# Moving operands of the large matmuls at one address modulo 256, in a two-block transformer kernel on one core

## The chip, the core and the metric

The kernel runs on one core of a Trainium2 chip. A core has TensorE (matmuls), VectorE, ScalarE, GpSimd, SyncE and 16 DMA engines. The metric is the time of one execution on the device, in microseconds (us).

## What is computed

Two blocks follow each other, all in float32. The input x is 256 rows of 2048. Both blocks, cut to what matters:

```python
# first block
mod = silu(c) @ w_ada + b_ada;  shift, scale, gate = split(mod, 3)
h = rms_norm(x, g_norm) * (1 + scale) + shift
qa, ka, va, za, q_idx, k_idx, w_idx, qb, kb, vb, zb = split(h @ w_in)   # 9296 columns
ya = selected_attention(qa, ka, va, q_idx, k_idx, w_idx)                 # top 64 keys
yb = causal_attention(qb, kb, vb)
y = concat(ya * silu(za), yb * silu(zb)) @ w_out
x = x + gate * y
# second block: 16 rows of meta tokens go ahead of x
z = rmsnorm(r, mix_pre_g) @ w_in_2 + b_in_2                              # 8200 columns
q, k, v, f_logit, u, g_attn, g_pool = split(z)
attn = forgetting_attention(q, k, v, log_sigmoid(f_logit))
pool = multiscale_pool(u, pool_w, pool_scale)
m = sigmoid(g_attn) * (attn @ w_attn_o) + sigmoid(g_pool) * (pool @ w_pool_o)
r = r + rmsnorm(m @ w_out_2, mix_post_g)
a = causal_dwconv(rmsnorm(r, ffn_pre_g) @ w_ffn_up, conv_w, conv_b)      # 3 taps, 2 x 5632
r = r + rmsnorm((gelu(gate) * val) @ w_ffn_down, ffn_post_g)             # gate, val = split(a)
out = r[16:]
```

The weights are 96 million numbers, 383 MB, and each is read once.

## The kernel before

**Activations are kept transposed**: a chunk holds 128 of the 2048 features on the partitions, and the rows of the sequence as columns. The first block works on SEQ = 256 columns, the second on ROWS = 272 (with the meta tokens) and, where the convolution's reach is all that is needed, on LIVE = 258, from column LIVE0 = 14 on.

**Each large product is done in three matmuls** of the type float32r. Weights and activations are split in a high part, which that type holds exactly, and the low rest. Lines 753 to 755 are the inner loop of `panel` in `pe_program`:

```python
pe.matmul(out, w_lo, a_hi, start=c == 0, stop=False)
pe.matmul(out, w_hi, a_lo, start=False, stop=False)
ins = pe.matmul(out, w_hi, a_hi, start=False, stop=last)
```

The weights are the stationary operand (128 x 128), the activations the moving one, of 256, 272 or 258 columns of 4 bytes. A **job** is one product. It has n panels of 512 output columns, and a panel has J pieces of weights, each 128 x 1024 (two chunks k of the contraction by 512 columns). For one piece, `panel` goes over four banks of PSUM (M.acc), and in each over the two chunks with three matmuls each: a panel of 16 chunks has 192 matmuls. The jobs in order: qidx0, strip, qidx1, qk_a, v_a, qk_b, v_b, z_a, z_b, out_a, out_b (256 columns); qkv2, f2, u2 (272); g2, attn_o, pool_w, attn_o3, pool_o, out2, up (258); down. The matmuls of pool_w are written out on lines 1053 to 1055. Between the pieces of qk_a to z_b and of g2 stand the small matmuls and transposes of the attention.

**The pieces** come by SyncE's DMAs into four tiles raw, in turn. ScalarE copies one to w_hi (line 1170), VectorE subtracts it for w_lo (line 1660), and TensorE gives the slot back when the piece is done. Semaphores count all of this; the order on each engine is written out by hand.

**The last product, down**, is the other way round: the activations (d_hi, d_lo) are stationary and the weight tiles move, with 512 columns, on lines 1121 to 1123 of `down_panel`.

**Where operands lie.** `memory` gives each tile its byte offset in a partition. What is worked out from it, modulo 256:

| tile | start | pitch of a chunk | chunks at, modulo 256 |
|---|---|---|---|
| w_hi, w_lo (four each) | 128 | 512 per bank, 2048 per k | 128 |
| act_hi, act_lo (all jobs but those below) | 128 | 1088 (272 columns) | 128, 192, 0, 64 in turn |
| the same, read by g2 from column 14 | 184 | 1088 | 184, 248, 56, 120 in turn |
| ya_hi, ya_lo (job out_a) | 64 | 1024 | 64 |
| o_hi / o_lo (attn_o, attn_o3) | 64 / 128 | 1032 | 8 more from chunk to chunk |
| down_hi, down_lo (job down, stationary) | 64 | 512 per matmul | 64 |

The pitch of act_hi is that of 272 columns in all jobs, whatever a job's own width.

Of the kernel before, what the change touches and what calls it, by code (L numbers as in the profile page):

```python
# [28 lines left out]
P = 128  # L29
# [22 lines left out]
PANEL = 512  # L52
POOL_WINDOWS = (2, 4, 8, 16)
# [103 lines left out]
def memory(nc, ctx, A):  # L157
# [50 lines left out]
    q0 = at["o"]  # L208
    M.region = q0


    ada_at = q0
# [46 lines left out]
    x += 16 * LIVE * 4 + 64  # L259
    x = (x + 31) // 32 * 32  # L260
# [14 lines left out]
    M.e8 = put("head_row", [HEADS, P], offset=z + 12288)  # L275
    M.fx = put("log_f", [HEADS, 2 * ROWS], offset=z + 12800)
# [126 lines left out]
    def act(k, c0=0, n=SEQ):  # L403
        return M.act_hi[:, ROWS * k + c0:ROWS * k + c0 + n], M.act_lo[:, ROWS * k + c0:ROWS * k + c0 + n]
# [11 lines left out]
    def attn(k):  # L416
# [726 lines left out]
def act_program(M, act):  # L1143
# [118 lines left out]
    def hi_of(k, c0=0, n=SEQ):  # L1262
        return M.act_hi[:, ROWS * k + c0:ROWS * k + c0 + n]
# [138 lines left out]
    def live_rstd(sem, count, src, c0, n):  # L1402
        def go():
# [5 lines left out]
                         "qkv2", ht(ROWS), lambda c: hi_of(c, 0, ROWS), source=32))  # L1409
# [237 lines left out]
def dve_program(M, dve):  # L1647
# [519 lines left out]
```

## Time and profile before

| | us |
|---|---|
| median of 3 runs | 2143.71 (2142.81 to 2145.34) |
| span of the profiled execution | 2141.7 |
| TensorE busy | 2010.6 (94%), 15084 matmuls |
| VectorE busy | 1282.3 (60%) |
| ScalarE busy | 991.1 (46%) |
| DMA | 391.62 MB, 183 GB/s on average |

The profile comes from one execution. Its rows are groups of instructions by source line, with the number of instructions, their busy time and the mean time of one. A matmul's duration runs from its start to its (modelled) end; matmuls overlap each other, so the time that one costs is the distance from its start to the next one's, and not its duration. "PE" is TensorE, "DVE" VectorE, "ACT" ScalarE, "SP" SyncE. Tile names come without their numbers.

### The profile page before, as it was taken

How to read it: one execution, taken by the hardware profiler on the slowest of the kernel's cores; microseconds unless marked ns; L12 is line 12 of the kernel's file. 1: busy time of each engine (PE TensorE's matmuls, PEld its weight loads, DVE VectorE, ACT ScalarE, POOL GpSimd, SP SyncE). 2: the span in 40 equal slices, each digit the busy share in tenths (PEclk: the TensorE clock that was granted, in tenths of full speed). 3: DMA queues.
4: the chain of work that ended last, by engine and by line, in shares of the span. 5: the costliest groups of instructions: out<-in, count | busy, mean ns of one | idle time of the engine just before them, and what ended most of it. 6: DMA issues, size and time to landing. Idle time of an engine off the chain costs nothing.

```text
span 2141.7 us, 39022 instructions
## 1 busy us (share of the span) xinstructions
PE 2010.6 (94%) x15084; PEld 1911.8 (89%) x15084; DVE 1282.3 (60%) x1565; ACT 991.1 (46%) x1429; POOL 143.8 (7%) x151
## 2 busy tenths in 40 slices
PE   4169999999999999999999999799999999999997
PEld 2169999999999899988899999699999999988886
DVE  6777885685567633444447664666556666664555
ACT  3034555554554444444344444454444444444443
POOL 0000000000002000000004111100000000000000
PEclk8579999999999999999999999899999999999999
DMA  8868665475555555644444555255655665665553
GB/s 308 307 192 286 224 196 175 137 251 182 158 168 188 156 171 157 185 145 138 146 137 142 189 189 179 78 177 174 189 178 175 185 186 177 189 204 189 193 190 124
DMA packets 179903, 391.62 MB, mean 183 GB/s; under 512 B 11955, under 2 KB 17632, under 8 KB 177376
## 3 DMA queue, kind: packets, MB, share of 16 engines
q1 hardware_dynamic: 178800, 388.03, 57.0%
q10 hardware_dynamic: 1024, 2.51, 0.3%
q8 instruction: 54, 0.88, 0.2%
q14 instruction: 25, 0.20, 0.0%
HBM read 388.39 MB, written 2.10 MB: 182 GB/s over the span
## 4 chain that ended last, share of the span: by engine, by line
PE 89%; DVE 4%; DMA 4%; ACT 2%; issue 1%; DVEq 0%; SPq 0%; POOLq 0%; POOL 0%; ACTq 0%
PE acc L753 20%; PE acc L755 20%; PE acc L754 20%; DMA raw<-in_w_ada 4%; PE psum_y L754 2%; PE psum_y L755 2%; PE psum_x L754 2%; PE psum_x L755 2%; PE psum_y L753 2%; PE psum_x L753 2%; PE acc L1123 2%; PE acc L1122 2%; PE acc L1121 2%; PE psum_y L1123 1%; PE psum_x L1123 1%
## 5 line engine op out<-in xcount | busy, mean ns | idle before, releaser
L1660 DVE TENSOR_TENSOR w_lo<-raw,w_hi 128x1024 fp32r<-128x1024 f32 (+1 forms) x644 | 814.0, 1271 | 727.2 <-ACT w_hi L1170 723.9
L1170 ACT ACTIVATE w_hi<-raw 128x1024 fp32r<-128x1024 f32 (+1 forms) x644 | 675.2, 1050 | 929.1 <-PE acc L755 602.4
L753 PE MATMUL acc<-act_hi,w_lo 128*128 128x258 f32 (+2 forms) x3424 | 983.5, 287 | 16.9 <-issue 9.3
L755 PE MATMUL acc<-act_hi,w_hi 128*128 128x258 f32 (+2 forms) x3424 | 974.9, 285 | 0.0
L754 PE MATMUL acc<-act_lo,w_hi 128*128 128x258 f32 (+2 forms) x3424 | 972.8, 284 | 0.0
L753 PEld LDWEIGHTS acc<-act_hi,w_lo 128*128 128x128 f32 x3424 | 651.9, 190 | 27.7 <-issue 26.2
L754 PEld LDWEIGHTS acc<-act_lo,w_hi 128*128 128x128 f32 x3424 | 650.4, 190 | 0.7 <-issue 0.5
L755 PEld LDWEIGHTS acc<-act_hi,w_hi 128*128 128x128 f32 x3424 | 650.7, 190 | 0.0
L754 PE MATMUL psum_y<-act_lo,w_hi 128*128 128x258 f32 x352 | 100.1, 284 | 0.0
L755 PE MATMUL psum_y<-act_hi,w_hi 128*128 128x258 f32 x352 | 100.0, 284 | 0.0
L754 PE MATMUL psum_x<-act_lo,w_hi 128*128 128x258 f32 x352 | 99.8, 284 | 0.0
L755 PE MATMUL psum_x<-act_hi,w_hi 128*128 128x258 f32 x352 | 99.8, 283 | 0.0
L753 PE MATMUL psum_y<-act_hi,w_lo 128*128 128x258 f32 x352 | 99.4, 282 | 0.0
L753 PE MATMUL psum_x<-act_hi,w_lo 128*128 128x258 f32 x352 | 99.3, 282 | 0.0
L1123 PE MATMUL acc<-w_hi,down_hi 128*128 128x512 f32 x176 | 69.3, 394 | 0.0
L1122 PE MATMUL acc<-w_lo,down_hi 128*128 128x512 f32 x176 | 69.0, 392 | 0.0
L1121 PE MATMUL acc<-w_hi,down_lo 128*128 128x512 f32 x176 | 68.3, 388 | 0.0
L716 POOL TENSOR_TENSOR ffn_act<-gelu_gate,conv_val 128x1024 f32 x11 | 34.5, 3135 | 503.5 <-DVE conv_val L1654 503.5
L753 PEld LDWEIGHTS psum_y<-act_hi,w_lo 128*128 128x128 f32 x352 | 67.2, 191 | 0.0
L755 PEld LDWEIGHTS psum_y<-act_hi,w_hi 128*128 128x128 f32 x352 | 66.9, 190 | 0.0
L754 PEld LDWEIGHTS psum_y<-act_lo,w_hi 128*128 128x128 f32 x352 | 66.8, 190 | 0.0
L755 PEld LDWEIGHTS psum_x<-act_hi,w_hi 128*128 128x128 f32 x352 | 66.8, 190 | 0.0
(291 smaller groups left out, 2186.6 us busy)
## 6 DMA issues: line engine op xcount, KB each, us to landing
raw<-in_w_in SPq DMA_DIRECT2D x272, 512.0 KB, 3.6
raw<-in_w_ffn_up SPq DMA_DIRECT2D x176, 512.0 KB, 3.9
raw<-in_w_ffn_down SPq DMA_DIRECT2D x88, 512.0 KB, 3.5
raw<-in_w_ada SPq DMA_DIRECT2D x64, 512.0 KB, 5.2
raw<-in_w_out SPq DMA_DIRECT2D x64, 512.0 KB, 4.1
ada_x<-in_w_ada SPq DMA_DIRECT2D x16, 1024.0 KB, 7.3
raw<-in_w_attn_o SPq DMA_DIRECT2D x16, 512.0 KB, 3.6
raw<-in_w_pool_o SPq DMA_DIRECT2D x16, 512.0 KB, 4.4
```

The lines of the kernel that those rows point to most:

```text
L716: pool.tensor_tensor(M.F[:, ds(i * 4 * SEQ, 4 * SEQ)], M.gg[:, :], M.vt[:, :], ALU.mult).then_inc(M.F_ready, 1)
L753: pe.matmul(out, w_lo, a_hi, start=c == 0, stop=False)
L754: pe.matmul(out, w_hi, a_lo, start=False, stop=False)
L755: ins = pe.matmul(out, w_hi, a_hi, start=False, stop=last)
L1121: pe.matmul(out, d_lo, w_hi, start=start, stop=False)
L1122: pe.matmul(out, d_hi, w_lo, start=False, stop=False)
L1123: ins = pe.matmul(out, d_hi, w_hi, start=False, stop=stop)
L1170: act.activation(M.hi[s][:, 0:job.width], M.raw[s][:, 0:job.width], ACT.Copy).then_inc(M.hi_ready[s], 1)
L1660: dve.tensor_tensor(M.lo[s][:, 0:job.width], M.raw[s][:, 0:job.width], M.hi[s][:, 0:job.width].bitcast(FP32), ALU.subtract).then_inc(M.lo_ ...
```

## The change

Only addresses change; every engine has the same instructions, in the same order, with the same waits. The activations no longer lie ahead of the constants but behind them, at the next offset that is 64 modulo 256. There are two layouts of the same space: act_hi and act_lo with a pitch of 1024 for the first block, act2_hi and act2_lo with a pitch of 320 columns, 1280 bytes, for the second. The stationary tiles of down move from 64 to 192 modulo 256. To make room, head_row and log_f move into parts of o_hi and o_lo. The scratch tiles of the second block shift by 64 bytes modulo 256 with that. g2 still reads its chunks from column 14 on.

```diff
+LINE = 256
+MOVING = 64
+STILL = 192
+PITCH = 320
...
-    act_at = at["o"]
-    M.act_hi = put("act_hi", [P, DC * ROWS], F32R)
-    M.act_lo = put("act_lo", [P, DC * ROWS], F32R)
-    M.ada_first = put("ada_first", [P, D], offset=act_at)
...
-    q0 = at["o"]
-    M.region = q0
-
-
-    ada_at = q0
+    act_at = (at["o"] + LINE - 1 - MOVING % LINE) // LINE * LINE + MOVING % LINE
+    M.act_hi = put("act_hi", [P, DC * SEQ], F32R, act_at)
+    M.act_lo = put("act_lo", [P, DC * SEQ], F32R, act_at + DC * SEQ * 4)
+    M.act2_hi = put("act2_hi", [P, DC * PITCH], F32R, act_at)
+    M.act2_lo = put("act2_lo", [P, DC * PITCH], F32R, act_at + DC * PITCH * 4)
+    M.ada_first = put("ada_first", [P, D], offset=act_at)
+
+
+    ada_at = act_at + 2 * DC * SEQ * 4
+    q0 = act_at + 2 * DC * PITCH * 4
...
-    x += 16 * LIVE * 4 + 64
-    x = (x + 31) // 32 * 32
+    M.e8 = put("head_row", [HEADS, P], offset=x + 6 * LIVE * 4 + 16)
+    M.fx = put("log_f", [HEADS, 2 * ROWS], offset=x + 14 * LIVE * 4 + 16)
+    x = (x + 14 * LIVE * 4 + 16 + 2 * ROWS * 4 + 31) // 32 * 32
...
-    M.d_hi = put("down_hi", [P, 4 * SEQ], F32R, x + 24576)
-    M.d_lo = put("down_lo", [P, 4 * SEQ], F32R, x + 28672)
-    x += 32768
+    d_at = x + 24576
+    d_at += (STILL - d_at) % LINE
+    M.d_hi = put("down_hi", [P, 4 * SEQ], F32R, d_at)
+    M.d_lo = put("down_lo", [P, 4 * SEQ], F32R, d_at + 4096)
+    x = d_at + 8192
...
-    def act(k, c0=0, n=SEQ):
-        return M.act_hi[:, ROWS * k + c0:ROWS * k + c0 + n], M.act_lo[:, ROWS * k + c0:ROWS * k + c0 + n]
+    def act(k):
+        return M.act_hi[:, SEQ * k:SEQ * k + SEQ], M.act_lo[:, SEQ * k:SEQ * k + SEQ]
+
+    def act2(k, c0, n):
+        return M.act2_hi[:, PITCH * k + c0:PITCH * k + c0 + n], M.act2_lo[:, PITCH * k + c0:PITCH * k + c0 + n]
...
-        Job("qkv2", 6, 8, cols(w_in2, 0), lambda k: act(k, 0, ROWS), ROWS),
+        Job("qkv2", 6, 8, cols(w_in2, 0), lambda k: act2(k, 0, ROWS), ROWS),
...
-        Job("g2", 8, 8, cols(w_in2, 4096 + HEADS), lambda k: act(k, LIVE0, LIVE), LIVE),
+        Job("g2", 8, 8, cols(w_in2, 4096 + HEADS), lambda k: act2(k, LIVE0, LIVE), LIVE),
...
-        Job("up", 22, 8, None, lambda k: act(k, 0, LIVE), LIVE),
+        Job("up", 22, 8, None, lambda k: act2(k, 0, LIVE), LIVE),
```

The other jobs of the second block, and the steps of ScalarE and VectorE that write the activations, take act2 in the same way.

## Rows read from the trace of the kernel before

**Rows 1.** The chain that ended last: shares of the span by engine.

```profile
PE 89%; DVE 4%; DMA 4%; ACT 2%; issue 1%; DVEq 0%; SPq 0%; POOLq 0%; POOL 0%; ACTq 0%
```

**Rows 2.** Windows: length, busy (instructions) of PE, PEld, DVE, ACT, POOL; PEclk, DMA, GB/s.

```profile
128.00:701.00 573.00, 568.02 (x4613) 551.62 (x4614) 392.60 (x516) 303.42 (x454) 33.22 (x33) 0.99 0.60 194
...
709.00:912.00 203.00, 202.24 (x1591) 201.86 (x1591) 93.18 (x98) 93.70 (x118) 4.34 (x10) 0.99 0.56 166
912.00:1151.00 239.00, 239.00 (x1782) 213.78 (x1782) 115.05 (x183) 102.55 (x176) 10.11 (x23) 1.00 0.48 142
...
1342.00:1370.00 28.00, 14.94 (x53) 11.34 (x53) 17.40 (x20) 12.76 (x32) 6.29 (x2) 0.73 0.15 49
1370.00:1886.00 516.00, 516.00 (x4256) 516.00 (x4256) 318.31 (x373) 250.49 (x298) 31.34 (x10) 1.00 0.59 179
```

**Rows 3.** Tile ya_hi: duration ns least/median/most, first and last start, forms.

```profile
L755 PE MATMUL acc<-ya_hi,w_hi x128: 276/276/276, 612.5 to 655.7; 128*128 128x256 f32 x128
```

**Rows 4.** Tile act_hi from 655.7 to 701.5 us (out_b), same columns.

```profile
L755 PE MATMUL acc<-act_hi,w_hi x128: 276/282/288, 656.0 to 701.1; 128*128 128x256 f32 x128
```

**Rows 5.** Groups of PE by shape: count, busy us, mean ns.

```profile
L754 PE MATMUL acc<-act_lo,w_hi 128*128 128x258 f32 x1600 | 454.7, 284 | 0.0
...
L754 PE MATMUL acc<-act_lo,w_hi 128*128 128x256 f32 x1296 | 365.3, 282 | 0.0
...
L754 PE MATMUL acc<-act_lo,w_hi 128*128 128x272 f32 x528 | 152.8, 289 | 0.0
L754 PE MATMUL psum_y<-act_lo,w_hi 128*128 128x258 f32 x352 | 100.1, 284 | 0.0
...
L754 PE MATMUL psum_x<-act_lo,w_hi 128*128 128x258 f32 x352 | 99.8, 284 | 0.0
```

**Rows 6.** Windows of TensorE alone: length, busy (instructions), granted clock, DMA, GB/s.

```profile
720.00:840.00 120.00, 120.00 (x955) 1.00 0.59 173
1500.00:1700.00 200.00, 200.00 (x1657) 1.00 0.61 183
1892.00:2118.00 226.00, 226.00 (x989) 1.00 0.55 188
```

**Rows 7.** Groups at 1501.67 us, job up: a chunk at 64; order 753, 754, 755.

```profile
L755 PE MATMUL psum_x<-act_hi,w_hi 128*128 128x258 f32 x1 | 0.3, 289 | 0.0
L754 PE MATMUL psum_x<-act_lo,w_hi 128*128 128x258 f32 x1 | 0.3, 283 | 0.0
L753 PE MATMUL psum_x<-act_hi,w_lo 128*128 128x258 f32 x1 | 0.3, 276 | 0.0
```

**Rows 8.** Groups at 1501.31 us, the chunk at 0 ahead of it.

```profile
L754 PE MATMUL psum_x<-act_lo,w_hi 128*128 128x258 f32 x1 | 0.3, 292 | 0.0
```

**Rows 9.** Line 754 in 1430:1530 and in 720:840 us: duration ns least/median/most.

```profile
L754 PE MATMUL acc<-act_lo,w_hi x149: 280/283/292, 1429.8 to 1529.8; 128*128 128x258 f32 x149
L754 PE MATMUL acc<-act_lo,w_hi x319: 282/287/293, 719.8 to 840.0; 128*128 128x272 f32 x160
```

**Rows 10.** Groups of PE: job down in its first banks.

```profile
L1123 PE MATMUL acc<-w_hi,down_hi 128*128 128x512 f32 x176 | 69.3, 394 | 0.0
L1122 PE MATMUL acc<-w_lo,down_hi 128*128 128x512 f32 x176 | 69.0, 392 | 0.0
L1121 PE MATMUL acc<-w_hi,down_lo 128*128 128x512 f32 x176 | 68.3, 388 | 0.0
L1123 PE MATMUL psum_y<-w_hi,down_hi 128*128 128x512 f32 x88 | 34.7, 394 | 0.0
L1123 PE MATMUL psum_x<-w_hi,down_hi 128*128 128x512 f32 x88 | 34.7, 394 | 0.0
```

**Rows 11.** Waits of TensorE: us in total, times, longest.

```profile
PE acc L753 <- DVE act_lo L1654: 5.7, 5, 3.8
...
PE psum_x L764 <- DVE prob L1848: 1.7, 3, 0.7
```

**Rows 12.** Timeline of TensorE: start us, duration us.

```profile
1501.42 0.28 PE L753 MATMUL psum_x<-act_hi,w_lo 128*128 128x258 f32 x1
1501.53 0.28 PE L754 MATMUL psum_x<-act_lo,w_hi 128*128 128x258 f32 x1
1501.65 0.29 PE L755 MATMUL psum_x<-act_hi,w_hi 128*128 128x258 f32 x1
1501.78 0.29 PE L753 MATMUL psum_y<-act_hi,w_lo 128*128 128x258 f32 x1
```

More of the change, by code:

```diff
@@ L432, in memory @@
         Job("out_b", 4, 4, cols(w_out, 0, 4), act, SEQ),
-        Job("qkv2", 6, 8, cols(w_in2, 0), lambda k: act(k, 0, ROWS), ROWS),
-        Job("f2", 1, 4, lambda i, j: w_in2_s[j][:, :, 3072:3200], lambda k: act(k, 0, ROWS), ROWS,
+        Job("qkv2", 6, 8, cols(w_in2, 0), lambda k: act2(k, 0, ROWS), ROWS),
+        Job("f2", 1, 4, lambda i, j: w_in2_s[j][:, :, 3072:3200], lambda k: act2(k, 0, ROWS), ROWS,
             4, 128, (3,)),
-        Job("u2", 2, 8, cols(w_in2, 3072 + HEADS), lambda k: act(k, 0, ROWS), ROWS),
-        Job("g2", 8, 8, cols(w_in2, 4096 + HEADS), lambda k: act(k, LIVE0, LIVE), LIVE),
+        Job("u2", 2, 8, cols(w_in2, 3072 + HEADS), lambda k: act2(k, 0, ROWS), ROWS),
+        Job("g2", 8, 8, cols(w_in2, 4096 + HEADS), lambda k: act2(k, LIVE0, LIVE), LIVE),
         Job("attn_o", 3, 4, cols(w_ao, 0), attn, LIVE),
-        Job("pool_w", 1, 4, lambda i, j: pool_w[j], lambda k: act(k, 0, LIVE), LIVE, 2, 256),
+        Job("pool_w", 1, 4, lambda i, j: pool_w[j], lambda k: act2(k, 0, LIVE), LIVE, 2, 256),
         Job("attn_o3", 1, 4, cols(w_ao, 3 * PANEL), attn, LIVE),
-        Job("pool_o", 4, 4, cols(w_po, 0), lambda k: act(8 + k, 0, LIVE), LIVE),
-        Job("out2", 4, 8, cols(w_out2, 0), lambda k: act(k, 0, LIVE), LIVE),
-        Job("up", 22, 8, None, lambda k: act(k, 0, LIVE), LIVE),
+        Job("pool_o", 4, 4, cols(w_po, 0), lambda k: act2(8 + k, 0, LIVE), LIVE),
+        Job("out2", 4, 8, cols(w_out2, 0), lambda k: act2(k, 0, LIVE), LIVE),
+        Job("up", 22, 8, None, lambda k: act2(k, 0, LIVE), LIVE),
         Job("down", 11, 8, lambda i, j: down[i, j // 2, j % 2], None, 512, 1, 1024, ()),
@@ L1260, in act_program, with hi_of, hi2_of @@
     ch.step(act.activation(M.bgate[:, :], M.c2[:, V2_UG + 8:V2_UG + 40], ACT.Copy, scale=0.5), wait=False)
-    def hi_of(k, c0=0, n=SEQ):
-        return M.act_hi[:, ROWS * k + c0:ROWS * k + c0 + n]
+    def hi_of(k):
+        return M.act_hi[:, SEQ * k:SEQ * k + SEQ]
+    def hi2_of(k, n):
+        return M.act2_hi[:, PITCH * k:PITCH * k + n]
     def stored(job, i, tile, func=ACT.Copy, squares=None):
@@ L1530, in act_program @@
     mx = pairs(8, "out2", lambda c: M.G[:, c * LIVE:(c + 1) * LIVE],
-               lambda c: hi_of(c, 0, LIVE), source=None, waits=m_done, scale=0.5)
+               lambda c: hi2_of(c, LIVE), source=None, waits=m_done, scale=0.5)
     panel(po, po.n - 1, {n: [mx[n]] for n in range(4)})
@@ L1700, in dve_program @@
     sq = lambda c: M.sq[:, (c % 4) * SEQ:(c % 4 + 1) * SEQ]
-    part_hi = lambda k, n=SEQ: M.act_hi[:, ROWS * k:ROWS * k + n].bitcast(FP32)
-    part_lo = lambda k, n=SEQ: M.act_lo[:, ROWS * k:ROWS * k + n]
+    part_hi = lambda k: M.act_hi[:, SEQ * k:SEQ * k + SEQ].bitcast(FP32)
+    part_lo = lambda k: M.act_lo[:, SEQ * k:SEQ * k + SEQ]
+    part2_hi = lambda k, n: M.act2_hi[:, PITCH * k:PITCH * k + n].bitcast(FP32)
+    part2_lo = lambda k, n: M.act2_lo[:, PITCH * k:PITCH * k + n]
     ch.step(dve.memset(M.ada_first[:, :], 0.0), wait=False)
```

20 lines of the change are left out of this document (9 added, 11 removed).

## The prediction

> **What bounds the kernel now.** I read the chain that ended last first: 89% of it is TensorE [rows 1]. Then the stages in a table of windows: from 128 us to the end of the last projection at 2127 us TensorE is busy nearly without a gap, at the full granted clock, while VectorE, ScalarE and the DMA engines work 60%, 50% and 60% of the time [rows 2]. No instruction is added, removed or reordered by the change, so what it can move is how fast one matmul follows another.
>
> The profile says what that spacing is. In the first half of the output projection (job out_a) the 128 matmuls of line 755 start from 612.5 to 655.7 us; between first and last lie 127 times three matmuls, so one takes 43.2 / 381 = 113.4 ns, and every one has a duration of 276 ns, least and most alike [rows 3]. The second half (out_b) runs the same loop over the same weight matrix, with the same 256 columns, and needs 45.1 / 381 = 118.4 ns, with durations from 276 to 288 [rows 4]. What differs in the code is where the moving operand lies. ya_hi and ya_lo start at 64 bytes modulo 256 and have a pitch of 1024, so each chunk is at 64. act_hi and act_lo start at 128 with a pitch of 1088, so chunk k is at 128, 192, 0, 64 in turn. The stationary operand is at 128 in both. I take this pair as the price of the address.
>
> The other widths, from counts per window (less what was under way at the left edge): 272 columns 120 us / 953 = 125.9 ns, 258 columns 200 / 1655 = 120.8 ns, 512 columns 226 / 988 = 228.7 ns [rows 6]. A duration exceeds its own spacing by about 163 ns (276 against 113.4), so durations in a small window show the spacing of single matmuls.
>
> **A rule against it.** The rows above say that 5 ns hang on the address alone. The Trainium skill says otherwise: its page "SBUF — State Buffer", section "Who interferes with whom", has it that "PE and ACT never wait on anyone", and "TensorE: Matmul & The Clock Gate", section "Step-by-step: what each phase is for", that loading the next weights takes no read bandwidth from the running matmul. By these an address would cost nothing and the sum below would be zero. The trace disagrees, with 276 ns at one address and 276 to 288 at the others.
>
> **Part by part.**
>
> (A) 256 columns, jobs qidx0 to z_b and out_b: pitch 1024, all chunks at 64. That is out_a's case exactly, stationary operand included. Lines 753 to 755 have 1296 each, 3888 in all [rows 5]. The 192 of qidx0 are fed by VectorE step by step (it waits 5.7 us for act_lo there [rows 11]) and gain nothing: 3696 x (118.4 - 113.4) = **18.5 us**. Bounds: none below 15 if the softmax steps between the panels take back some. TensorE's waits for them are 1.7 us now [rows 11], which speaks for the full sum. Above: 19.4.
>
> (B) 272 columns, jobs qkv2, f2, u2: pitch 1280, all at 64: 3 x 528 = 1584 matmuls [rows 5]. The clean value worked out from out_a is 113.4 + 16 columns at 2.4 GHz = 120.1 ns. A 272-column matmul can come that low: the least duration of line 754 is 282 ns (276 + 6.7 is 282.7), its median 287 [rows 9]. 1584 x (125.9 - 120.1) = **9.2 us**; the lower bound is 2 us, if only one in four or five becomes clean.
>
> (C) 258 columns at 64: jobs pool_w, pool_o, out2 and up. The rows of line 754 with this form count 1600 + 352 + 352; less 512 of g2 and with 16 of pool_w on a line of its own that is 1808, times three 5424 matmuls [rows 5]. This is the term on which the result hangs, since a clean value of 113.4 + 0.8 = 114.2 ns would give 5424 x 6.6 = 35.8 us. The trace has this very case already in every fourth chunk (act at 64, weights at 128), and there it isn't clean throughout: the three matmuls of such a chunk take 276, 283 and 289 ns [rows 7], from 1501.42 to the next start at 1501.78, 0.36 us for the three [rows 12]. A chunk at 0 has up to 292 ns [rows 8]. The last of the three may suffer from the next chunk's address, and the first gain from the one before; the middle one has neighbours at 64 on both sides, as in out_a, and takes 283 where out_a's takes 276. It is no exception: of 149 matmuls of line 754 with 258 columns, a quarter of them at 64, none was under 280 ns [rows 9]. Two columns more than 256 seem to cost a step of their own. Its start and the next are 1501.53 and 1501.65 [rows 12], and 283 less 163 is 120, so I take 119.5 ns: 5424 x 1.3 = **7.1 us**. Ends for the range: 114.2 ns (35.8 us) and no gain.
>
> (D) 512 columns, job down: the moving operand is the weight tile, at 128 as before; the stationary one goes from 64 to 192. Line 1123 has 176 + 88 + 88, and with its two sisters that is 1056 [rows 10]. In out_a moving minus stationary is 64 - 128 = -64. Here it is +64 now and becomes 128 - 192 = -64. If only the difference counts, a matmul takes out_a's 113.4 plus 256 columns at 2.4 GHz, 220.1 ns: 1056 x (228.7 - 220.1) = **9.1 us**. Durations of 388 to 394 ns with nothing below [rows 10], where 276 + 106.7 would be 383, say that none is clean now. No row shows a stationary operand at 192, so the bounds are 0 and 9.1. I take the full value, by analogy with out_a alone.
>
> (E) Job g2 reads its chunks from column 14 on, so they lie at 64 + 56 = 120 and not at 64: 1536 matmuls. Before, a quarter of them lay at 120 as well, and the median of all 258-column rows is the same 283 ns [rows 9]. I take nothing, with bounds of 5 us either way. attn_o keeps its pitch of 1032: nothing.
>
> (F) Moved tiles: constants now lie ahead of the activations, head_row and log_f inside o_hi and o_lo. Waits and their order are unchanged, so nothing. The cover: when TensorE takes 1 to 5% less per panel, the weight pieces must come as much faster. With VectorE at 62% and the DMA engines at 59% in the longest stage [rows 2] they do. What lies ahead of 128 us and the stall at 1342 to 1370 us stay as they are.
>
> **Sum:** 18.5 + 9.2 + 7.1 + 9.1 = 43.9 us. The profiled execution has a span of 2141.7 us, the median of the runs is 2143.7; taking the sum from either, with the 2.0 us outside the span kept, gives **2100 us**.
>
> **The rivals.**
>
> R1, 258 columns run clean as well, because the 283 and 289 are remnants of the chunk at 0 ahead and of the one behind, and only a long run at one address settles. For it: out_a settles in one state, and 276 does occur for 258 columns. Against it: the middle one. 43.9 + 28.7 = 72.6 us, 2071 us. Chance 0.22.
>
> R2, only the exact case of out_a gains: (A) 18.5 and a part of (B) and (D), 258 columns nothing. 15 to 30 us, around 2120 us. Chance 0.14.
>
> R3, the address isn't the cause: out_a is clean for another reason (what the other engines read and write meanwhile). 2144 us. [...] Against it: ScalarE and VectorE split the same weight pieces in out_b. Chance 0.07.
>
> R4, slower. With 258 columns a fixed address can hold TensorE in its worst state instead of passing through it once in four chunks. The place is job up; the price is that of the worst row, 292 ns or about 130 ns of spacing [rows 8]: 5424 x 9.2 = 50 us lost against 37 won elsewhere, 2156 us. It decides from about 127.6 ns on. Chance 0.06.
>
> **Numbers.** The forecast, 2090 to 2112 us with the bounds of (A), (B) and (D), holds 0.51, R1 0.22, R2 0.14, R3 0.07, R4 0.06. Likeliest: 2100. The range takes in R1 with (E)'s bound and nearly all of R2: 2062 to 2131, which leaves out R3, R4 and little more. Faster by over 0.2% (4.3 us, about what a measurement of this kernel can tell from no change) 0.87, within 0.2% 0.06, slower 0.07.
>
> **What would show it.** (A) Lines 753 to 755 with 256 columns at 276 ns throughout, and panels of v_a or out_b at 113.4 ns. (B) 283 ns instead of 287 to 291. (C) one repeated pattern for 258 columns; whether it is 276, 283 or above decides between forecast, R1 and R4. (D) 383 ns on lines 1121 to 1123. (E) g2 unchanged. If PE gets idle time before line 753 instead, my claim on the cover is wrong.

## The result

| | before | changed |
|---|---|---|
| median, us | 2143.26 (2141.08 to 2145.34, 4 runs) | 2127.25 (2125.42 to 2129.99, 4 runs) |
| profiled execution: span, us | 2141.7 | 2123.6 |

The ratio is 0.9926, with a 95% interval of 0.9912 to 0.994: 16 us faster. The forecast was 2100 us, so 44 us were promised and a little over a third came. The 2127 us lie in the stated range, but that was made wide enough (2062 to 2131) to take in two rivals. The kernel is faster, but by the medians nearer to rival R2 (2120) than to the forecast.

### The profile after

Lines 753, 754 and 755 of before are 762, 763 and 764 here, and 1121 to 1123 are 1130 to 1132. The chain that ended last still is TensorE, with the same share as in [rows 1]:

```profile
PE 89%; DVE 4%; DMA 4%; ACT 2%; issue 1%; DVEq 0%; SPq 0%; POOLq 0%; POOL 0%; ACTq 0%
```

The windows by stage, columns as in [rows 2]: the 256-column jobs, the 272-column jobs, g2, attn_o to out2, the pause ahead of up, up, and the larger part of down:

```profile
127.00:687.00 560.00, 554.31 (x4615) 537.66 (x4616) 392.56 (x516) 302.35 (x454) 34.29 (x33) 0.99 0.62 199
694.00:894.00 200.00, 198.79 (x1589) 198.26 (x1590) 93.88 (x100) 93.41 (x118) 4.33 (x10) 0.99 0.59 169
894.00:1132.00 238.00, 238.00 (x1789) 212.74 (x1788) 115.62 (x183) 103.15 (x177) 10.70 (x23) 1.00 0.49 143
1132.00:1323.00 191.00, 190.61 (x1580) 190.43 (x1579) 115.25 (x134) 93.65 (x138) 45.80 (x42) 1.00 0.55 180
1323.00:1348.00 25.00, 11.95 (x46) 8.81 (x44) 16.44 (x18) 11.94 (x30) 6.30 (x2) 0.86 0.15 44
1348.00:1864.00 516.00, 516.00 (x4259) 515.91 (x4260) 319.00 (x376) 250.84 (x299) 31.22 (x10) 1.00 0.60 179
1870.00:2100.00 230.00, 230.00 (x988) 185.30 (x987) 115.83 (x126) 99.89 (x125) 0.10 (x1) 1.00 0.56 184
```

Set beside [rows 2]: the same matmuls of the first stage (x4615 and x4613) need 560 us and not 573; the 272-column stage 200 and not 203; g2 238 and not 239; up is where it was, 516 us. In down, 988 matmuls take 230 us, where before 989 took 226 [rows 6].

The two traces by stage, from the first start of a matmul of each job to the first of the next stage (spacing is the mean distance from one start to the next within a stage; gaps of over 200 ns, the waits, are left out):

| stage | before, us | changed, us | difference | spacing before, changed, ns |
|---|---|---|---|---|
| ahead of the first job | 128.2 | 127.0 | -1.2 | |
| 256 columns | 572.9 | 559.8 | **-13.1** | below |
| gap behind them | 7.6 | 7.6 | 0 | |
| qkv2, f2, u2 (272) | 202.9 | 199.4 | -3.5 | 126.0, 123.4 |
| g2 (258) | 239.5 | 237.6 | -1.9 | 120.4, 119.1 |
| attn_o to out2 | 191.7 | 191.6 | -0.1 | 120.9, 120.8 |
| pause | 26.8 | 25.0 | -1.8 | |
| up (258) | 516.3 | 515.3 | -1.0 | 120.8, 120.8 |
| down (512) and the end | 255.8 | 260.3 | **+4.5** | 228.9, 233.3 |
| sum | | | -18.1 | |

Within the first stage: qk_a 118.5 to 113.4, v_a 118.7 to 113.4, v_b 118.8 to 113.5, but qk_b 118.9 to 115.4, z_a 118.9 to 115.4, z_b 119.1 to 115.3, out_b 118.2 to 117.8, and **out_a 113.4 to 117.8**.

Not all of the 18.1 us is spacing. Within z_a the kernel before has the granted clock of TensorE at the lower of its two levels (1.2 GHz, half of 2.4) for 3.4 us; the changed kernel has not. Length, busy, instructions, clock, DMA, GB/s, before, then changed:

```profile
508.00:511.50 3.50, 3.50 (x19) 0.52 0.21 81
```

```profile
496.00:510.00 14.00, 14.00 (x122) 1.00 0.44 133
```

From its first start to its last z_a takes 55.2 us in the two executions without such a dip (this one and live144 below), 56.6 in four of the five with one of 3.4 us, and 58.2 in the two with one of 6.8 us. So some 1.4 of the 13.1 us are the clock's. The pause ahead of up had a mean clock of 0.73 before [rows 2] and has 0.86 here, and the 1.8 us there go with it: the 32 matmuls that sum the squares take 453 ns on average for 523. The 1.2 us ahead of the first job are no gain that can be told from scatter: in the kernels below that stretch takes 126.0 to 128.5 us.

out_a is the surprise. Its addresses are the same modulo 256 in both kernels. Tile ya_hi, columns as in [rows 3], then tile act_hi in the time of out_b, as in [rows 4]:

```profile
L764 PE MATMUL acc<-ya_hi,w_hi x128: 281/281/281, 596.7 to 641.6; 128*128 128x256 f32 x128
...
L764 PE MATMUL acc<-act_hi,w_hi x128: 281/281/281, 641.9 to 686.8; 128*128 128x256 f32 x128
```

In [rows 3] it was 276/276/276. So the same pair of addresses, moving at 64 and stationary at 128, has a second pattern, 281 ns and (641.6 - 596.7) / 381 = 117.8 ns, which is as steady as the first.

Where it comes from can be read in the same trace. z_b, the job ahead of out_a, reads its moving operand at 64 too, and its last piece is in this slow pattern already:

```profile
L764 PE MATMUL acc<-act_hi,w_hi x7: 281/281/281, 593.9 to 596.0; 128*128 128x256 f32 x7
```

The first matmul of out_a follows 118 ns behind the last of z_b, with nothing between. So out_a takes over the pattern that z_b ended in, and hands it on to out_b. In the kernel before, z_b went from place to place (118.1 to 120.3 ns by piece), and out_a was at 113.4 ns from its third matmul on.

Line 763, duration least/median/most: 272 columns in 720 to 840 us, then the 258 columns of up (three tiles of output), then g2:

```profile
L763 PE MATMUL acc<-act_lo,w_hi x322: 285/286/288, 720.0 to 838.8; 128*128 128x272 f32 x161
...
L763 PE MATMUL acc<-act_lo,w_hi x149: 280/283/289, 1407.8 to 1507.9; 128*128 128x258 f32 x149
L763 PE MATMUL psum_x<-act_lo,w_hi x64: 280/282/283, 1422.7 to 1490.5; 128*128 128x258 f32 x64
...
L763 PE MATMUL acc<-act_lo,w_hi x436: 278/281/285, 929.8 to 1129.7; 128*128 128x258 f32 x146
```

272 columns have become even (285 to 288 where [rows 9] has 282 to 293) and a little faster, but do not reach the prediction's clean value (282.7). 258 columns run through a repeated pattern with the old median. Last, down, to set beside [rows 10] (388, 392, 394):

```profile
L1131 PE MATMUL acc<-w_lo,down_hi 128*128 128x512 f32 x176 | 69.6, 396 | 0.0
L1132 PE MATMUL acc<-w_hi,down_hi 128*128 128x512 f32 x176 | 69.6, 396 | 0.0
L1130 PE MATMUL acc<-w_hi,down_lo 128*128 128x512 f32 x176 | 69.6, 395 | 0.0
```

TensorE's waits between the panels have hardly moved (for act_lo 5.5 us, for prob 2.1; 5.7 and 1.7 in [rows 11]):

```profile
PE acc L762 <- DVE act_lo L1666: 5.5, 4, 3.8
...
PE psum_x L773 <- DVE prob L1862: 2.1, 3, 0.9
```

### The profile page after: what moved, and what is told of

Read it like the earlier page. It is cut to its first block, busy times and chain, and to the rows that moved or that the text cites. A ratio compares the mean times of both kernels' runs of the same rounds, so it can differ in the third digit from the quotient of the medians.

```text
span 2123.6 us, 39022 instructions
## 1 busy us (share of the span) xinstructions
PE 1992.5 (94%) x15084; PEld 1889.5 (89%) x15084; DVE 1281.7 (60%) x1565; ACT 989.7 (47%) x1429; POOL 144.6 (7%) x151
## 3 DMA queue, kind: packets, MB, share of 16 engines
q10 hardware_dynamic: 1024, 2.51, 0.3%
## 4 chain that ended last, share of the span: by engine, by line
PE 89%; DMA 4%; DVE 4%; ACT 2%; issue 1%; DVEq 0%; SPq 0%; POOLq 0%; POOL 0%; ACTq 0%
PE acc L762 20%; PE acc L763 20%; PE acc L764 20%; DMA raw<-in_w_ada 4%; PE psum_y L763 2%; PE psum_x L762 2%; PE psum_x L764 2%; PE psum_y L762 2%; PE psum_y L764 2%; PE psum_x L763 2%; PE acc L1130 2%; PE acc L1132 2%; PE acc L1131 2%; PE psum_y L1130 1%; PE psum_x L1130 1%
## 5 line engine op out<-in xcount | busy, mean ns | idle before, releaser
L763 PEld LDWEIGHTS psum_x<-act_lo,w_hi 128*128 128x128 f32 x352 | 67.1, 191 | 0.0
```

## The experiments

The theory from here on: **TensorE disturbs itself**. What a matmul costs hangs on its width and on the places modulo 256 of its two operands, and at some pairs a run settles in one of two lasting patterns. Rival: other engines' reads and writes do it. The runs can show what the cost hangs on; what happens inside the chip none of them shows.

### Undo the last projection's address

```diff
-STILL = 192
+STILL = 64
```

> The change with down's stationary tiles back at 64 modulo 256 and nothing else undone. Theory 1 (the spacing of a matmul depends on the distance between its moving and its stationary operand): lines 1130 to 1132 go from 395 and 396 ns back to 388, 392 and 394, the spacing from 233 to 229 ns, and 1056 matmuls give 4.7 us: about 2122.5 us. Rival (the trace of the change is off in down for another reason, such as the state in which the job is entered): the durations stay at 395, and the time at 2127.

Measured: 2125.46 us (2122.83 to 2128.54, 5 runs), ratio 0.9915 (0.9902 to 0.9929). The lines of down are back at the old durations, here of 1892 to 2118 us:

```profile
L1132 PE MATMUL acc<-w_hi,down_hi 128*128 128x512 f32 x160 | 63.0, 394 | 0.0
L1131 PE MATMUL acc<-w_lo,down_hi 128*128 128x512 f32 x159 | 62.3, 392 | 0.0
L1130 PE MATMUL acc<-w_hi,down_lo 128*128 128x512 f32 x159 | 61.7, 388 | 0.0
```

By the spacings this stage gained (233.3 - 228.9) x 1056 = 4.6 us, but the medians differ by 1.8 and the span is even longer (2124.9). In the trace the stage from down on is 4.5 us shorter (255.7 for 260.2); the reason for the span stands in earlier stages that the edit does not touch. TensorE in 720 to 820 us (length, busy, instructions, clock, DMA, GB/s), the changed kernel, then this one:

```profile
720.00:820.00 100.00, 100.00 (x813) 1.00 0.63 183
```

```profile
720.00:820.00 100.00, 100.00 (x791) 1.00 0.59 178
```

In this execution qkv2 ran at 126.3 ns, with the same addresses that gave 123.4 in the other, which cost 3.3 us; z_a took 1.3 us more with a dip of the clock. By pieces, qkv2 began at 123.3 here as well. Between its sixth and seventh piece both traces have a short hold (a distance of some 315 ns and one of 200); behind it this one ran at 126.7 to the end of the job, the other at 123.3. So 272 columns have more than one pattern too, and the addresses alone do not decide which is taken.

### A small matmul after each piece of weights

In out_a and out_b, after each of the four pieces of a panel:

```diff
-        panel(o, 0, acts=M.mk[name])
+        def kick():
+            pe.matmul(M.X[:, 1000:1016], ident[:, :], ones[:, 0:16], start=True, stop=True)
+        panel(o, 0, {j: [kick] for j in range(4)}, acts=M.mk[name])
...
-            panel(o, i + 1)
+            panel(o, i + 1, {j: [kick] for j in range(4)})
```

> The change with one more small matmul (16 columns, into a part of PSUM that nobody reads) after each piece of out_a and out_b, 32 in all. In the change all 768 matmuls of these two jobs take 281 ns (117.8 ns of spacing), at the same address at which they took 276 before. Theory 1 (with 256 columns at this address there are two lasting patterns, and only a break in the stream of matmuls chooses between them): after each break the matmuls of a piece are at 276 or at 281 throughout, some pieces change over, and the jobs become up to 3.4 us shorter, less some 0.1 us for each break. Rival (281 ns is what these jobs cost with this layout, because of what else lies where): all pieces stay at 281, and the kernel is 2 to 3 us longer.

Measured: 2132.7 us (2132.03 to 2139.0), ratio 0.9961 (0.9947 to 0.9974), so 5 us slower than the changed kernel. Yet the matmuls are in the fast pattern:

```profile
L764 PE MATMUL acc<-ya_hi,w_hi x128: 276/276/282, 599.4 to 646.1; 128*128 128x256 f32 x128
...
L764 PE MATMUL acc<-act_hi,w_hi x128: 276/276/276, 646.7 to 693.2; 128*128 128x256 f32 x128
```

The 24 matmuls ahead of the first small one were slow; from then on all were fast (113.9 and 113.4 ns on average). The job still takes 46.9 us from first to last start where the slow pattern had 45.1, since each small matmul costs some 0.2 us. Sixteen breaks a job cost more than they are worth: the two jobs together take 94.1 us for 90.3. Of the rest, 3 us are a dip of the clock in z_a (58.2 us for 55.2), ahead of the edit. Only the first of the 32 small matmuls met the slow pattern and turned it; the other 31 met the fast one and left it as it was.

### TensorE alone

No model is computed. The three matmuls of the inner loop are repeated to a run of 36 instructions, six times for each width and pair of places, and the other engines are idle meanwhile:

```python
pe.matmul(acc[b][:, 0:cols], w_lo, hi, start=True, stop=False)
pe.matmul(acc[b][:, 0:cols], w_hi, lo, start=False, stop=False)
ins = pe.matmul(acc[b][:, 0:cols], w_hi, hi, start=False, stop=True)
```

> TensorE alone: runs of 36 matmuls in the kernel's order of operands (low weights by high activations, high by low, high by high), each at one fixed pair of addresses modulo 256, 6 runs for a pair, with a break of varying length ahead of each. Widths 256, 258 and 272 with the moving operand at 0, 32 to 224 and the stationary one at 128; 256 and 258 also at (0, 64), (128, 192), (192, 0); width 512 with the moving one at 128 and the stationary one at 0 to 224. The other engines are idle, and what is computed isn't the reference. Theory 1 (TensorE's two reads disturb each other, by the distance of their addresses): the durations depend on the pair of addresses as in the kernel: 256 at 64 has 276 or 281, 258 at 64 has 280 to 289, 512 at (128, 64) has 388 to 394 and at (128, 192) 393 to 398, and pairs of the same distance agree. Rival (the disturbance comes from ScalarE, VectorE and the DMAs, which are idle here): every pair takes 276 (256 columns), 277 (258), 283 (272) and 383 ns (512).

Measured, mean distance of the last 18 starts of each run, stationary operand at 128 (for 512 columns the moving one at 128, and the column head is the stationary one's place). The very first run, with matmuls 213 ns apart at its start, is left out:

| columns | 0 | 32 | 64 | 96 | 128 | 160 | 192 | 224 |
|---|---|---|---|---|---|---|---|---|
| 256 | 118.9 | 117-120 | **113.3** (4 of 6), 117.8 (2 of 6) | 118.4 | 120.0 | 116.4-117.8 | 117.8 | 120.0 |
| 258 | 120-122.2 | 120.1 | 120.6-120.9 | 120.0 | 120.0-121.2 | 119.8 | 118.7-122.2 | 120.0 |
| 272 | 126.7 | 123.3 | 123.3 | 125.3-126.7 | 125.3 | 125.3-125.9 | 126.7 | 125.4-126.7 |
| 512 | 232.7-233.3 | 233.3 | 228.9 | 233.3 | **226.7** | 233.3 | 233.3 | 234.4 |

Line 115, duration least/median/most: 256 columns with both at 128, and with moving at 0, stationary at 64; then 512 columns, moving at 128, stationary at 64, 128, 192:

```profile
L115 PE MATMUL acc<-m128e,s128e x72: 277/283/283, 150.4 to 179.5; 128*128 128x256 f32 x72
...
L115 PE MATMUL acc<-m000e,s064e x72: 276/276/286, 763.5 to 791.4; 128*128 128x256 f32 x72
...
L115 PE MATMUL acc<-m128e,s064e x72: 387/392/398, 1050.8 to 1103.2; 128*128 128x512 f32 x72
...
L115 PE MATMUL acc<-m128e,s128e x72: 387/389/396, 1159.3 to 1211.4; 128*128 128x512 f32 x72
...
L115 PE MATMUL acc<-m128e,s192e x72: 392/394/398, 1267.6 to 1320.8; 128*128 128x512 f32 x72
```

The numbers of the stages that keep to one place turn up with nothing else at work: 113.3 and 117.8, 120.8, 123.3, 228.9 and 233.3. The rival falls as the cause of them. The pairs (0, 64), (128, 192) and (192, 0), of the same distance as (64, 128), gave 113.3 in 18 of 18 starts. And for 512 columns distance 0 is the best, with both the old pair (128, 64) and the new one (128, 192) behind it.

The Trainium skill, "SBUF — State Buffer", section "Who interferes with whom", says that "PE and ACT never wait on anyone". These runs agree as far as they go: no other engine is needed for 256 columns to cost 113.3 or 120.0 ns. But a page on who waits for whom does not say that TensorE's own cost is one value, as the prediction had read it. The Trainium skill, "TensorE: Matmul & The Clock Gate", section "Step-by-step: what each phase is for", says that loading the next weights takes no read bandwidth from the running matmul. These runs, where the place of the weights alone moves 512 columns from 226.7 to 234.4 ns, show that the stream is not independent of the weights' place; by which way they disturb it no run shows.

### Widths, finer places, and the pairs again

The same program with 30 matmuls a start and 8 starts a group.

> Leaves the whole model out: only TensorE works, in groups of 30 matmuls that begin anew 8 times each, at chosen widths and addresses. Why are 258 and 272 columns never clean, while 256 are? Clean means the best value of 256 columns, 113.3 ns, plus or minus 0.417 ns a column. Theory 1, a matmul is disturbed as soon as its moving row is longer than 256 columns (1024 bytes): at moving 0, stationary 64 the widths 240, 248, 254, 256 take 106.6, 110.0, 112.5, 113.3 ns, and 258 to 320 all lie 3 to 7 ns above their clean 114.1 to 140.0. Theory 2, the row's end has to fall on a multiple of 16 columns (64 bytes): 240, 256, 272, 288, 304, 320 are clean and the others not. Theory 3, the length has to fit the period of the two reads, and 256 is the one that does: 254 and 240 are not clean either. For 256 columns with the moving operand at 40 to 88 and the stationary one at 128: if any place in a 64-byte piece will do, 113.3 at 64 to 88 and 117 to 120 at 40 to 56; if one distance alone is good, 113.3 at 64 only. The last four groups repeat pairs of the run before: 113.3 in 8 of 8 where the stationary one is not at 128, both 113.3 and 117.8 at moving 64, stationary 128. For 512 columns: if only the distance counts, (0,0), (64,64), (192,192) take 226.7 ns as (128,128) did, and (64,0) takes 228.9.

Measured at the pair (0, 64); the clean value is an estimate, 113.3 ns plus 0.417 (one cycle at 2.4 GHz) for each column over 256, or less, under it. From 288 to 320 columns the rows rise by 13.4 / 32 = 0.42:

| columns | 240 | 248 | 254 | **256** | 258 | 260 | 264 | 270 | 272 | 288 | 304 | 320 |
|---|---|---|---|---|---|---|---|---|---|---|---|---|
| ns | 112-113.3 | 116.6 | 118.2 | **113.3** | 120.8 | 120.0 | 120.2 | 124.4-126.7 | 123.3 | 133.3 | 138.8 | 146.7 |
| above the clean value of its width | 5.4-6.7 | 6.6 | 5.7 | 0 | 6.7 | 5.0 | 3.5 | 5.2-7.5 | 3.3 | 6.7 | 5.5 | 6.7 |

Theories 1 and 2 of this run both fall: 254 columns, at 118.2 ns, take more than 256, and 240 or 320, multiples of 16, are not clean. Of these widths only 256 is, as theory 3 has it, at this pair. The moving operand at 40 to 88 against 128 gave 113.3 at 64 alone, and 117 to 121 at the others. For 512 columns (0, 0), (64, 64) and (192, 192) all took 226.7 and (64, 0) 228.9, as in the run before (0, 64) took the 233.3 of (128, 192): there the distance is what counts. They have lasting patterns too, at (0, 16) 226.7 in 3 of 8 starts and 233.3 in 5. The four pairs repeated for 256 columns were 8 of 8 fast at (0, 64), but 6, 7 and 6 of 8 at (64, 128), (128, 192) and (192, 0). So 18 of 18 before was chance for two of the three pairs, and the third, (0, 64), shows the slow pattern in a kernel below.

### The last projection at distance 0

```diff
-STILL = 192
+STILL = 128
```

> The changed kernel with one number more: the stationary operand of the last product at 128 modulo 256, the address of its moving operand (distance 0), in place of 192. Theory 1, the distance between the two operands counts and 0 is the best for 512 columns, as with TensorE alone (226.7 ns): 1056 x (233.3 - 226.7) = 7.0 us less than the changed kernel, about 2120 us, with durations of 389 to 390 ns on the three lines of the last product; the rest of the kernel as in the changed one but for the two lasting patterns, which can move 3 us either way. Theory 2, with the other engines at work the value with TensorE alone isn't reached: 228.9 or more, 2122.6 us or slower.

Measured: 2123.12 us (2119.8 to 2125.75, 4 runs), ratio 0.9908 (0.9891 to 0.9925), span 2118.0. The spacing of down is 220 / 971 = 226.6 ns, and all three lines have 389:

```profile
1880.00:2100.00 220.00, 220.00 (x972) 1.00 0.55 184
...
L1132 PE MATMUL acc<-w_hi,down_hi 128*128 128x512 f32 x164 | 63.8, 389 | 0.0
L1130 PE MATMUL acc<-w_hi,down_lo 128*128 128x512 f32 x164 | 63.8, 389 | 0.0
L1131 PE MATMUL acc<-w_lo,down_hi 128*128 128x512 f32 x164 | 63.8, 389 | 0.0
```

Theory 1 holds for the stage, which takes 253.4 us for 260.2. Of these 7 us the medians show 4.1 and the spans 5.6; 1.4 us are lost in z_a, where this execution has the clock's dip and the changed kernel's has not.

### Everything moved by 64

```diff
-MOVING = 64
-STILL = 192
+MOVING = 0
+STILL = 64
...
-    base = 16512
+    base = 16704
```

> The changed kernel with all tiles moved so that the moving operands of the large products lie at 0 and the stationary ones at 64 modulo 256, and in the last product both at 64; the distance of moving to stationary stays at -64, in the last product it becomes 0. Theory 1, at this pair a run of 256-column matmuls has one pattern alone (113.3 ns in all 6 restarts with TensorE alone, where the pair 64 and 128 had 117.8 in 2 of 6): out_a and out_b take 113.4 ns instead of 117.8 (768 x 4.4 = 3.4 us), qk_b, z_a and z_b 113.4 instead of 115.4 (1536 x 2.0 = 3.1 us), the last product 226.7 to 228.9 instead of 233.3 (4.6 to 7.0 us); 272 columns lose 1584 x 2.5 = 4 us if they come to the 125.8 that they had there alone. Sum 7 to 10 us less than the changed kernel: 2117 to 2120 us. Theory 2, which of two patterns is taken hangs on what the other engines and the breaks do and not on the pair: out_a and out_b stay at 117.8 and the gain is the last product's alone, 2121 to 2126 us.

Measured: 2120.81 us (2119.65 to 2121.77, 4 runs), ratio 0.9892 (0.9876 to 0.9909), span 2119.3.

```profile
L764 PE MATMUL acc<-ya_hi,w_hi x128: 281/281/281, 598.9 to 643.7; 128*128 128x256 f32 x128
```

out_a is in the slow pattern at this pair as well, as is out_b. The time lies between the two forecasts, but the pattern decides for theory 2: the gain is down's, at 226.7 ns, and 272 columns stay at 123.4. The 125.8 of the expectation belongs to no run at this pair; with TensorE alone 272 columns take 123.3 at (0, 64).

### One small matmul, and places in steps of 8 bytes

Three kernels belong here. The first is TensorE alone again; in its last groups there is one more matmul halfway through the 36.

> Leaves the whole model out: only TensorE works, in groups of 36 matmuls that begin anew 4 times (10 in the last groups). The stationary operand is at 128 modulo 256 throughout; the moving one goes through all places in steps of 8 bytes, with 258 and with 272 columns. Theory 1, 258 columns are disturbed at every place: nothing below 118.5 ns, the best places some 1.5 ns below the 120.8 of the kernel (120, where the chunks of g2 now lie, has 119.1). Rival, there is a place where they are clean, 114.2 to 116 ns, which steps of 32 bytes have missed. For 272 columns likewise: 123.3 at best, or near 120.0 somewhere. The last seven groups have 256 columns at 64 and 128 and, after half of the run, one small matmul of 0, 16, 16, 32, 64, 128 or 256 columns. Theory 1, a break chooses anew between 113.3 and 117.8 ns: both patterns turn up on both sides of it, in 2 to 4 of 10 halves the slow one. Rival, a break always leads into 113.3 ns.

258 columns, stationary at 128, 32 places of the moving operand: 118 to 122 ns nearly everywhere, 123.3 at 232, and two that are lower in 4 of 4 starts, 117.8 at 248 and **116.7 at 144** (lower ones came once in 4 at 208, 116.7, and at 24 and 104, 117.8). The expectation of nothing below 118.5 missed that; the rival's clean 114 to 116 isn't there either. Line 143 at 64, then at 144:

```profile
L143 PE MATMUL acc<-moving,still x48: 280/283/289, 178.9 to 198.0; 128*128 128x258 f32 x48
...
L143 PE MATMUL acc<-moving,still x48: 277/280/288, 380.4 to 399.1; 128*128 128x258 f32 x48
```

272 columns: 123.3 at 32, 64 and 240 is the least that comes in every start. Elsewhere it is 124.4 to 129, but for single starts at 123.1 to 123.3 (places 40, 48, 112 and 168).

Of the small matmuls, those of 16, 32, 64 or 128 columns had the fast pattern ahead of them and behind them in 50 of 50 cases. So they do not throw a run out of it; that one turns slow to fast no case of this run tests. One of 256 columns (in plain float32, two instructions in the trace) met the fast pattern 4 times and left the slow one each time; of the 6 times that it met the slow one, the slow one stayed in 5. The timeline of TensorE around such a one (start us, duration us):

```profile
1634.65 0.28 PE L144 MATMUL acc<-moving,still 128*128 128x256 f32 x1
...
1636.01 0.28 PE L144 MATMUL acc<-moving,still 128*128 128x256 f32 x1
1636.13 0.59 PE L139 MATMUL acc<-src 128*128 128x256 f32 x2
1636.37 0.47 PE L142 MATMUL acc<-moving,still 128*128 128x256 f32 x1
...
1636.91 0.28 PE L142 MATMUL acc<-moving,still 128*128 128x256 f32 x1
...
1638.56 0.28 PE L144 MATMUL acc<-moving,still 128*128 128x256 f32 x1
```

Ahead of it 12 distances in 1.36 us, 113.3 ns; behind it 14 in 1.65 us, 117.9. "A break chooses anew, in 2 to 4 of 10 the slow one" was wrong here, and so was "a break always leads into the fast one": what stands in the break matters. It does not decide alone. In the changed kernel six transposes stand ahead of four pieces of qk_b, always with the fast pattern before them, and behind them two pieces run at 113.3 ns and two at 117.8. Nor does it take a matmul: behind two distances of some 160 and 220 ns in v_b, with nothing between, seven of the nine kernels with one place for 256 columns go on at 113.3 ns, and two (zero64 and both144) at 117.8 to the end of the job.

The second kernel has one small matmul after the first piece of out_a, and down at distance 0:

```diff
+        def kick():
+            pe.matmul(M.X[:, 1000:1016], ident[:, :], ones[:, 0:16], start=True, stop=True)
...
+        panel(o, 0, {0: [kick]} if name == "out_a" else {}, acts=M.mk[name])
```

> The changed kernel with the last product's stationary operand at 128 and one small matmul of 16 columns more, after the first piece of weights in out_a. Theory 1, the slow pattern of out_a and out_b (117.8 ns) is one that lasts until something breaks the stream, and the break chooses anew; in the run with a break after every piece all choices fell on 113.4 ns. So one break should turn the other 744 matmuls: 744 x 4.4 = 3.3 us less than the same kernel without it (2123.1 us), for 0.2 us of its own: about 2120 us, out_a with 24 matmuls at 117.8 and the rest at 113.4. Theory 2, the slow pattern comes back by itself, and only many breaks kept it away: out_b at 117.8 again and no gain, 2123 us.

```profile
L764 PE MATMUL acc<-ya_hi,w_hi x128: 276/276/283, 600.0 to 643.6; 128*128 128x256 f32 x128
...
L764 PE MATMUL acc<-act_hi,w_hi x128: 276/276/276, 643.9 to 687.1; 128*128 128x256 f32 x128
```

Measured: 2120.36 us (2118.97 to 2122.1, 4 runs), ratio 0.9896 (0.988 to 0.9913). One break turns out_a from its 25th matmul on and all of out_b: theory 1. From the first start of out_a to the last of out_b 87.3 us pass, 90.3 without it. With kick and both144 this makes three cases in which 16 columns turned the slow pattern to the fast one, and none in which they did not. The medians differ by 2.8 us, but with intervals that overlap, so the gain is shown in the trace and only likely in the time.

The third reads and writes the 258-column activations from column 14, at 120 modulo 256, also with down at distance 0:

```diff
-        Job("up", 22, 8, None, lambda k: act2(k, 0, LIVE), LIVE),
+        Job("up", 22, 8, None, lambda k: act2(k, LIVE0, LIVE), LIVE),
```

> The changed kernel with the last product's stationary operand at 128, and with the 258-column activations of pool_w, pool_o, out2 and up written and read from column 14 of each chunk on, as g2 reads them: the moving operand lies at 120 modulo 256 in place of 64. Theory 1, the place sets the price of 258 columns too, though it never makes them clean, and 120 has 119.1 ns (g2 in the changed kernel, and TensorE alone) where 64 has 120.8: (384 + 768 + 4224) x 1.7 = 9.1 us less than the same kernel without it (2123.1 us), about 2114 us, and no longer waits of VectorE or ScalarE for the odd place. Theory 2, g2 is fast for another reason (other banks, the attention between its panels) and up stays at 120.8 ns: 2123 us.

Measured: 2119.66 us (2119.46 to 2121.02, 4 runs), ratio 0.9892 (0.9876 to 0.9909). pool_o and out2 run at 119.0 and 119.1 ns, as forecast, but up takes a third value, 120.0, and holds it for 4060 of its 4224 matmuls:

```profile
L763 PE MATMUL acc<-act_lo,w_hi x150: 282/282/282, 1408.0 to 1507.7; 128*128 128x258 f32 x150
```

The place sets the price, and again there is more than one lasting pattern. Of the 9.1 us of theory 1 the medians show 3.5 (2123.1 to 2119.7). pool_o, out2 and up won 4.2 us from first to last start, and the pause ahead of up grew from 25.0 to 27.3 us, with a mean clock of 0.74 in it where still128 has 0.80.

### 258 columns at 144

As above, with `LIVE_AT = 20` in place of LIVE0: column 20 of a chunk lies at 144. Once with down at distance 0 alone, once with the one small matmul in out_a too.

> As the run with 258 columns read from column 14, but from column 20 of each chunk on (jobs pool_w, pool_o, out2 and up): the moving operand lies at 144 modulo 256. With TensorE alone this was the best of 32 places for 258 columns, 116.7 ns in 4 of 4 restarts, where 64 had 120.8 and 120 had 119.0. Theory 1, the place's price holds in the kernel, too: (384 + 768 + 4224) x (120.8 - 116.7) = 22 us less than the same kernel with them at 64 (2123.1 us), about 2101 us. Theory 2, in the kernel another of the lasting patterns is taken, as up took 120.0 ns at place 120 where pool_o and out2 took 119.0: 1152 x 4.1 + 4224 x 0.8 = 8 us, about 2115 us. Theory 3, TensorE isn't the only bound at that pace, since up wants its weights 3.4% sooner: waits of TensorE for w_lo of some us in up, between the two.

Measured: **2101.93 us** (2099.22 to 2105.41, 5 runs), ratio 0.9809 (0.9796 to 0.9823), 41 us faster than before and 25 than the changed kernel. All of up, and line 763 there:

```profile
1345.00:1844.00 499.00, 499.00 (x4256) 499.00 (x4257) 318.20 (x374) 249.36 (x298) 31.99 (x10) 0.99 0.62 185
...
L763 PE MATMUL acc<-act_hi,w_lo x158: 277/278/280, 1407.9 to 1507.7; 128*128 128x258 f32 x158
```

4256 matmuls in 499 us, where the changed kernel has 4259 in 516: 116.7 ns for 120.8, the value with TensorE alone to the tenth. TensorE is busy throughout, so the weights came in time; theories 2 and 3 fall, the waits for weights that theory 3 asked for are not there. Against the same kernel with them at 64 (still128) the medians differ by 21.2 us, where theory 1 had 22. The pause ahead of up takes 26.8 us here, as in the kernel before, at a mean clock of 0.72.

> The one with 258 columns at 144 modulo 256 (from column 20 on), and one small matmul of 16 columns after the first piece of weights in out_a, as before. The two touch different stages, so their gains add: out_a and out_b at 113.4 ns in place of 117.8, 87.3 us from the first start to the last in place of 90.4, 3 us less than the same kernel without the small matmul: about 2098 us by theory 1 of that run and 2112 by theory 2. If the small matmul is no switch, and the run with it fell on the good pattern by luck, out_a and out_b are at 117.8 after it here.

Measured: 2101.3 us (2099.71 to 2104.01, 5 runs), ratio 0.9803 (0.979 to 0.9816). The 3 us of out_a and out_b are there again in the trace (87.3 us for 90.3), and 276 ns on ya_hi. They are not in the time: in this execution v_b ran at 116.3 ns (113.8 in the one without) and z_a took 58.3 us from first to last start (55.2), stages ahead of the edit. z_a is the clock's doing, as these windows of both144 and live144 show (columns as above):

```profile
496.00:503.40 7.40, 7.40 (x38) 0.54 0.24 71
```

```profile
496.00:503.00 7.00, 7.00 (x62) 1.00 0.16 36
```

## Why the prediction was wrong

The mechanism was right, that the address sets the spacing and the spacing the time; the sum was wrong. **The step that failed** is to take out_a's 276 ns (113.4 ns of spacing) for the settled price of its address, and to carry it over to 272 and 258 columns by adding columns, and to 512 by taking over the distance. The runs showed in its place two lasting patterns at that pair of addresses, 113.3 and 117.8 ns, and a price table of its own for each width: at the changed kernel's places 123.3 ns for 272 columns, 120.8 for 258 and 233.3 for 512. Term by term:

**What bounds the kernel** held: same chain, same waits of TensorE, and about 14 of the 18.1 us lie in the spacing of matmuls; the rest is the clock's dip in z_a (1.4), the pause (1.8) and the start (1.2). Rival R3, that the address isn't the cause, is out.

**(A)** The price was right: 118.7 became 113.4 in v_a, and as much in qk_a and v_b. The stage gained 13.1 us and not 18.5. The 276 ns of out_a was the fast one of two patterns of that pair. In the changed kernel out_a itself lost 384 x 4.4 = 1.7 us and out_b gained 0.2 and not 1.9. In qk_b and z_b, where pieces after a break ran in either pattern, the jobs got shorter by 1.6 and 1.2 us where 5.0 ns a matmul would make 3.8 and 1.9. That is 6.4 short. z_a had the same mix of patterns, 384 x 3.5 = 1.3 us, but came to 2.7 with the clock's 1.4, 0.8 over its 1.9. The other jobs are within 0.2 us of the forecast.

**(B)** 3.5 us in the stage and not 9.2. No place of 32 gave 272 columns the clean 120.1: 123.3 is the least that came in every start. I took the least duration of a mixed distribution, 282 ns, for the level of a settled one; single matmuls came that low in [rows 9] while the mean was 126.

**(C)** Nothing and not 7.1: 120.8 stayed 120.8. The reading that 258 columns are not clean at 64 was right, and kept R1 from being the forecast. The 119.5 that I took was below what the rows gave (283 - 163 = 120), and the row at hand was one matmul; the mean over its neighbours was the number to use. The lower bound, no gain, was the value.

**(D)** is the largest miss: +4.5 us and not -9.1. "If only the difference counts" was true for 512 columns, but I carried over which difference is good, from 256 columns to 512. The good one there is 0 (226.7 ns), +64 was second (228.9), and -64 is among the bad (233.3). The bounds, 0 and 9.1, left out a loss, though no row showed a stationary operand at 192.

**(E)** 1.9 us of gain, within the bounds, and not foreseen. Alone, 258 columns take 119.0 ns at 120, as g2 does now (119.1); but the four places before, 184, 248, 56 and 120, average 119.1 alone as well (119.4, 117.8, 120.1, 119.0), where g2 took 120.4. So going from place to place seems to have cost something of its own, which no run took apart. **(F)** held for the waits; "stay as they are" did not for the pause, 1.8 us shorter at a higher clock.

The sum by these terms: 13.1 + 3.5 + 0 - 4.5 + 1.9 = 14.0 us where 43.9 stood; 1.2 ahead of the first job, 1.8 in the pause, 1.0 in up's stage and 0.1 make it the 18.1 by which the spans differ. R2, only the exact case gains, was the nearest rival, partly by luck: its (A) came in at 13.1 and not 18.5, and (D) was a loss, which put the changed kernel above its 2120. R1 falls as it was put: at 64 258 columns are not clean. But much of its size was real, and lay at another place: 144, which made 21 us by the medians where R1 had 28.7. R4's mechanism does exist (down held in a bad state), not in up but where I had seen no risk.

What stays open: what in the hardware makes the patterns, and what decides which one a run is in behind a break. Where the slow one of out_a comes from is known one step back: in all nine kernels that have z_b at one place, z_b's last piece runs at 117.8 ns, and out_a starts in it. Why z_b ends so in all nine, and qkv2 changed over in one execution, is open.

## What to carry over

Where TensorE alone sets the time, the distance between the starts of matmuls is worth a table of its own: width, place of the moving and of the stationary operand modulo 256, measured with the engine alone for exactly the width in use. Such a table held in the kernel to 0.1 ns in most stages (116.7, 226.7, 123.3), with other patterns in a few (126.7 at the place of 123.3, 120.0 in up at 120), and no value of one width said anything on another here. A steady duration in the trace (276/276/276) proves a pattern, not a law of the address: look for the same case elsewhere in the trace with another value before it goes into a sum.

## What was unexpected of the hardware

- The cost of a float32r matmul depends on where both operands lie, with all other engines idle: 256 columns 113.3 to 121.5 ns, 258 columns 116.7 to 123.3, 272 columns 123.1 to 129, 512 columns 226.7 to 234.4.
- 256 columns are a special case at the pair (0, 64): 254 columns take 118.2 ns and 258 take 120.8, where 256 take 113.3.
- At one pair of addresses two patterns, 113.3 and 117.8 ns, each last for hundreds of matmuls. It is handed on from job to job while nothing comes between (z_b to out_a to out_b). A float32 matmul of 16 columns turned the slow one to the fast one in 3 of 3 cases, those of 16 to 128 columns kept the fast one in 50 of 50, and one of 256 columns turned it to the slow one in 4 of 4.
- A float32 matmul of 16 to 128 columns between large ones costs 0.23 to 0.24 us in the stream with TensorE alone, more than a large one of 256 (0.113).
